# Decoder step with product-key experts: the value table taken one half of the width after the other, every product with w_hi on 448 columns, the first half's sums added midway

## What is computed

```python
def one(hx):                     # 128 rows at a time
    ...                          # top 16 of 128 x 128 product keys for 8 heads -> eidx, g = softmax(top)
    a = gelu(einsum('nd,nhkd->nhk', hx, u_tab[eidx]))
    w = (g * a)
    return einsum('nhk,nhkd->nd', w, v_tab[eidx])      # v_tab has 16384 rows of 1024
```

## Time and profile before

| | |
|---|---|
| three timed runs | 1252.82, 1248.13, 1249.46 us |
| profiled execution | 1249.17 us |
| its span, first to last instruction | 1247.5 us |
| TensorE busy | 1224.7 us, 98% |
| VectorE busy | 791.0 us, 63% |
| ScalarE busy | 623.3 us, 50% |
| GpSimd busy | 437.9 us, 35% |
| granted TensorE clock, mean | 0.991 |

### The profile page before, as it was taken

The page is one execution under the profiler, slowest core; times in us unless marked ns, Lnnn a source line. Parts: engine busy times, 40 slices in busy tenths (PEclk is TensorE's granted clock), DMA queues, the critical chain, the costliest instruction groups (busy, mean ns, idle before and its releaser), DMA issues.

```text
span 1247.5 us, 24718 instructions
## 1 busy us (share of the span) xinstructions
PE 1224.7 (98%) x9143; PEld 1141.2 (91%) x9143; DVE 791.0 (63%) x1425; ACT 623.3 (50%) x1265; POOL 437.9 (35%) x436
## 2 busy tenths in 40 slices
PE   7999999999999999999999999999999999999998
PEld 5688898978899999999999999999989898988988
DVE  6445565655784999997667777544555455545455
ACT  5333464532553544457777777544544444444443
POOL 3430325441000688883000000000556565565630
PEclk9999898999999999999999999999999999999999
DMA  8661836664655356565444444455788788888883
GB/s 324 209 202 53 129 124 221 222 204 140 203 193 167 108 159 184 160 181 165 137 144 130 141 135 137 147 175 182 285 263 304 266 301 273 295 275 291 287 281 121
DMA packets 104808, 246.90 MB, mean 198 GB/s; under 512 B 36080, under 2 KB 48432, under 8 KB 103984
## 3 DMA queue, kind: packets, MB, share of 16 engines
q1 hardware_dynamic: 78672, 190.51, 47.4%
q0 software_dynamic: 18752, 51.40, 12.5%
q10 hardware_dynamic: 7264, 3.40, 1.2%
HBM read 237.79 MB, written 11.64 MB: 200 GB/s over the span
## 4 chain that ended last, share of the span: by engine, by line
PE 89%; issue 2%; POOL 2%; DVE 2%; ACT 1%; SPq 1%; DMA 1%; ACTq 0%; DVEq 0%
PE ps L1975 23%; PE ps L1980 12%; PE ps L2065 9%; PE ps L2057 9%; PE ps L1539 5%; PE ps L2059 5%; PE ps L2060 4%; PE ps L2029 4%; PE ps L2078 2%; POOL w_lo L534 2%; PE ps L1792 2%; PE ps L1685 1%; PE ps L1559 1%; PE ps L1654 1%; PE ps L1647 1%
## 5 line engine op out<-in xcount | busy, mean ns | idle before, releaser
L882 ACT ACTIVATE w_hi<-ring 128x1024 fp32r<-128x1024 f32 x280 | 296.8, 1060 | 382.7 <-issue 212.8
L1338 DVE TENSOR_TENSOR w_lo<-ring,w_hi 128x1024 fp32r<-128x1024 f32 x232 | 283.9, 1224 | 278.1 <-ACT w_hi L882 278.1
L1975 PE MATMUL ps<-h_hi,w_hi 128*128 128x288 f32 x1088 | 299.9, 302 | 0.5 <-ACT w_hi L882 0.5
L1975 PE MATMUL ps<-h_lo,w_hi 128*128 128x288 f32 x1024 | 278.7, 296 | 0.0
L1975 PEld LDWEIGHTS ps<-h_hi,w_hi 128*128 128x128 f32 x1088 | 204.9, 188 | 1.2 <-ACT w_hi L882 1.0
L1975 PEld LDWEIGHTS ps<-h_lo,w_hi 128*128 128x128 f32 x1024 | 192.7, 188 | 0.0
L534 POOL TENSOR_TENSOR w_lo<-ring,w_hi 128x1024 fp32r<-128x1024 f32 x48 | 133.5, 2795 | 146.9 <-ACT w_hi L882 146.6
L550 POOL DMA_INDIRECT arena<-act_kept,aux x64 | 64.7, 1011 | 321.7 <-DMA act_kept<-arena 302.5
L543 POOL DMA_INDIRECT arena<-in_v,aux x128 | 134.6, 1051 | 111.4 <-PE ps L2078 76.4
L1980 PE MATMUL ps<-h_hi,w_lo 128*128 128x288 f32 x1088 | 166.7, 295 | 2.1 <-POOL w_lo L534 1.8
L1980 PEld LDWEIGHTS ps<-h_hi,w_lo 128*128 128x128 f32 x1088 | 152.5, 188 | 3.4 <-POOL w_lo L534 3.0
(11 more groups left out here) (361 smaller groups left out, 2287.9 us busy)
## 6 DMA issues: line engine op xcount, KB each, us to landing
ring<-in_uT SPq DMA_DIRECT2D x128, 512.0 KB, 3.6
ring<-in_v SPq DMA_DIRECT2D x128, 512.0 KB, 4.6
ring<-in_wout SPq DMA_DIRECT2D x32, 512.0 KB, 3.3
ring<-in_wT SPq DMA_DIRECT2D x28, 512.0 KB, 4.2
ring<-in_wtok SPq DMA_DIRECT2D x8, 512.0 KB, 4.0
arena<-in_cache_slc_v POOLq DMA_DIRECT2D x64, 64.0 KB, 2.9
act_kept<-arena SPq DMA_DIRECT2D x32, 128.0 KB, 3.8
arena<-in_cache_cmp_k POOLq DMA_DIRECT2D x48, 64.0 KB, 3.1
```

Of the source, the lines that this page charges most:

```text
L882: act.activation(w_hi[e % 2][:, :], ring[:, (W_O + e) % RING, :], ACT.Copy).then_inc(S["w_high"], 1)
L1338: dve.tensor_tensor(w_lo[e % 2][:, :], ring[:, (W_O + e) % RING, :], w_hi[e % 2][:, :].bitcast(F32), ALU.subtract)\
L1975: last = pe.matmul(ps[:, bank, 0:NT], w_hi[e % 2][:, k * P:(k + 1) * P], mov[:, k, :], start=(k == 0 and mov is mov_hi), stop=False, skip_ ...
```

## The change

Tile t now has dh = t // 64 and pp = t % 64: all 64 tiles of the left half of the width first, then all 64 of the right half. The right half's sums use banks 0 to 3 with 448 columns each, in place of two shared banks; banks 2 and 3 hold sums of the left half (m = 0 and 1), which are therefore added to `xT` in tile 64. Each tile has a moving operand of its own, so `mov_high` and `mov_low_part` are called for every tile, and tile t uses buffer t % 2. Cut to its core:

```diff
-VSUM = (((2, 0), (3, 0), (4, 0), (5, 0)), ((0, 0), (0, ND), (1, 0), (1, ND)))
+VBANK = ((2, 3, 4, 5), (0, 1, 2, 3))
 def v_tile(t):
-    pp, dh = t // 2, t % 2
+    pp, dh = t % HALF, t // HALF
...
             for a, b in ((0, 4), (4, 6), (6, 7), (7, 8)):
-                sp.wait_ge(S["y_ready"], b)
+                sp.wait_ge(S["y_ready"], b + 1)
...
-            def mov_high(pp):
-                if pp >= 2:
-                    act.wait_ge(S["lo_used"], E_V + 2 * (pp - 2) + 2)
-                    act.wait_ge(S["mov_low"], pp - 1)
-                act.activation(mov_parts[pp % 2][:, :, 0, :], rows[:, 2 * pp:2 * pp + 2, :], ACT.Copy).then_inc(S["mov_high"], 1)
+            def mov_high(t):
+                pp = t % HALF
+                if t >= 2:
+                    act.wait_ge(S["lo_used"], E_V + t - 1)
+                    act.wait_ge(S["mov_low"], t - 1)
+                act.activation(mov_parts[t % 2][:, :, 0, :], rows[:, 2 * pp:2 * pp + 2, :], ACT.Copy).then_inc(S["mov_high"], 1)
...
             act.wait_ge(S["tile_weighed"], PK - ROUTE_AT)
+            mov_high(1)
             for t in range(2, PK):
-                if t % 2 == 0:
-                    mov_high(t // 2)
+                mov_high(t)
                 w_high(E_V + t)
...
+            def add_sums(dh, ms):
+                for m in ms:
+                    dve.wait_ge(S["lo_used"], E_V + (HALF if dh == 0 else PK - 1 + m + 1))
+                    x = xT[:, 4 * dh + m, 0:ND]
+                    link(dve.tensor_tensor(x, x, ps[:, VBANK[dh][m], ND:2 * ND], ALU.add))
+                    dve.tensor_tensor(x, x, ps[:, VBANK[dh][m], 0:ND], ALU.add).then_inc(S["y_ready"], 1)
+            mov_low_part(1)
             for t in range(2, PK):
-                if t % 2 == 0:
-                    mov_low_part(t // 2)
+                if t == HALF + 1:
+                    dve.wait_ge(S["x1_back"], 32)
+                    add_sums(0, (0, 1))
+                mov_low_part(t)
                 w_low_part(E_V + t)
+                if t == HALF + 1:
+                    add_sums(0, (2, 3))
...
+            last.then_inc(S["y_ready"], 1)
+            add_sums(1, range(4))
...
                 pe.wait_ge(S["w_high"], e + 1)
-                pe.wait_ge(S["mov_low"], pp + 1)
-                for h in range(2):
-                    for m, (bank, c0) in enumerate(VSUM[dh]):
...
-                        pe.matmul(ps[:, bank, c0:c0 + ND], w, both[h][:, 0:ND], start=first, stop=False, skip_group_check=True)
-                        last = pe.matmul(ps[:, bank, c0:c0 + ND], w, both[h][:, ND:2 * ND], start=False, stop=False, skip_group_check=True)
+                pe.wait_ge(S["mov_low"], t + 1)
+                if t == HALF:
+                    high((0, 1))
+                    low_done(pe, e)
+                    low(0)
+                    low(1)
+                    pe.wait_ge(S["y_ready"], 2)
+                    high((2, 3)).then_inc(S["hi_used"], 1)
+                    low(2)
+                    low(3).then_inc(S["lo_used"], 1)
+                    return
+                high(range(4)).then_inc(S["hi_used"], 1)
...
-                if t == 1:
+                if t == HALF:
                     pe.wait_ge(S["u_done"], PK)
                     pe.wait_ge(S["tile_weighed"], PK - ROUTE_AT)
```

More of the change, by code:

```diff
@@ L1483, in weigh_tile, with mov_low_part @@
                 dve.tensor_tensor(rows[:, j, 0:cut], ps[:, j % 2, 0:cut], rows[:, j, 0:cut], ALU.mult).then_inc(S["tile_weighed"], 1)
[L1485 to L1490, removed]
+            def mov_low_part(t):
+                pp = t % HALF
+                dve.wait_ge(S["mov_high"], t + 1)
+                if t >= 2:
+                    dve.wait_ge(S["hi_used"], E_V + t - 1)
+                dve.tensor_tensor(mov_parts[t % 2][:, :, 1, :], rows[:, 2 * pp:2 * pp + 2, :], mov_parts[t % 2][:, :, 0, :].bitcast(F32), ALU.subtract)\
                     .then_inc(S["mov_low"], 1)
@@ L1522, in _ @@
                 new = ps[:, 6 + dh, :].rearrange("p (k q c) -> p k c q", k=4, q=GRP)[:, :, 0:EGROUPS, :]
[L1523 to L1531, removed]
+                last = dve.tensor_tensor(x, x, new, ALU.add)
+            last.then_inc(S["y_ready"], 1)
+            add_sums(1, range(4))
         @block.tensor
@@ L2045, in value_tile @@
             def value_tile(t):
-                pp, dh = t // 2, t % 2
+                dh = t // HALF
                 e = E_V + t
-                both = [mov[pp % 2][:, 2 * h * ND:2 * h * ND + 2 * ND] for h in range(2)]
-                pe.wait_ge(S["w_high"], e + 1)
-                pe.wait_ge(S["mov_low"], pp + 1)
-                for h in range(2):
-                    for m, (bank, c0) in enumerate(VSUM[dh]):
[L2054 to L2058, removed]
-                        pe.matmul(ps[:, bank, c0:c0 + ND], w, both[h][:, 0:ND], start=first, stop=False, skip_group_check=True)
-                        last = pe.matmul(ps[:, bank, c0:c0 + ND], w, both[h][:, ND:2 * ND], start=False, stop=False, skip_group_check=True)
@@ L2061, in value_tile, with high @@
-                last.then_inc(S["hi_used"], 1)
+                both = [mov[t % 2][:, 2 * h * ND:2 * h * ND + 2 * ND] for h in range(2)]
+                def high(ms):
+                    for h in range(2):
+                        for m in ms:
+                            last = pe.matmul(ps[:, VBANK[dh][m], 0:2 * ND], w_hi[e % 2][:, h * 512 + m * P:h * 512 + (m + 1) * P], both[h],
+                                             start=(t % HALF == 0 and h == 0), stop=False, skip_group_check=True)
+                    return last
@@ new lines, in low @@
+                def low(m):
+                    for h in range(2):
+                        last = pe.matmul(ps[:, VBANK[dh][m], 0:ND], w_lo[e % 2][:, h * 512 + m * P:h * 512 + (m + 1) * P], both[h][:, 0:ND],
+                                         start=False, stop=(t % HALF == HALF - 1 and h == 1), skip_group_check=True)
+                    return last
+                pe.wait_ge(S["w_high"], e + 1)
+                pe.wait_ge(S["mov_low"], t + 1)
[9 more added lines that the diff above has]
+                    return
@@ L2062, in value_tile @@
+                high(range(4)).then_inc(S["hi_used"], 1)
                 low_done(pe, e)
[L2063 to L2066, removed]
+                for m in range(4):
+                    last = low(m)
```

## The result

The changed kernel takes 1237.75 us, the median of 8 runs (1231.56 to 1243.01); the kernel before, run beside it, 1248.18 (1243.33 to 1252.82, 8 runs). The ratio is 0.992, with a 95% interval of 0.989 to 0.995: faster by 0.8%, 10.4 us between the medians. The forecast was 1241.9 us, between 1240.3 and 1246.0. The direction was right; the time lies 2.5 us under the range. The times alone couldn't tell a gain of 10.4 us from the forecast one of 7.3: that would be a ratio of 0.994, inside the interval. The traces can.

A forecast was written before the change was run, and what follows sets the result against it. TensorE's stream of matmuls was taken to set the pace. From one execution of 1249.17 us: - 8.8 (saving) + 0.6 (first tile) + 0.7 (tile 64) + 0.2 (end) = 1241.9 us, range for 8 in 10 1240.3 to 1246.

The forecast's parts named there:

- What bounds the kernel: Value stage: TensorE's stream of matmuls sets the pace, so what counts is the time from start to start.
- The saving: Right half's 64 tiles: merging 224-column matmuls into 448 saves 0.137 us a tile, 8.8 us in all, bounds 8.3 to 9.0.
- The fixed part of a matmul: Value stage matmuls: each costs 0.016 us besides its columns; the change takes 8 of these from each of 64 tiles.
- no fixed part: Rival, right half: the 0.111 us come from elsewhere, 448 columns keep 1.78 us; 1250.7 us, no change; chance 0.03.
- What is added in every tile: 62 more mov_high on ScalarE and 62 more mov_low on VectorE, covered by the tile before: cost nothing.
- First tile: Start of the value stage: tile 1 waits for its own mov_low after the last u tile's weighing; +0.6 us, bounds 0.5 to 0.9.
- tile 64: Between the halves: TensorE waits for two pairs of additions; +0.7 us, bounds 0.5 to 2.2.
- End: After tile 127's first w_lo matmul: later additions +0.8 us, stores -0.6; sum +0.2, bounds -0.3 to +0.8.
- The term for the stores: End of the span: 576 KB leave early, last store lands in 2.7 us; 2.9 us follow the last addition instead of 3.5, -0.6.
- Sum: Whole kernel: 1249.17 - 8.8 + 0.6 + 0.7 + 0.2 = 1241.9 us; with bounds 1240.9 to 1244.8.
- The Trainium skill's formula: Start to start of matmuls: 95.8 ns for 224 columns, 189.2 for 448; merging 512 pairs would save 1.2 us in all.
- the prediction's rival of the late ring: Rival, SP's tile loads: a load over 7.8 us delays a tile; one in ten late by 0.5 us gives 1248; chance 0.04.

The follow-up runs named there:

- e10: Changed kernel with w_hi of the right half in two matmuls of 224 columns instead of one of 448: 1249.1 against 1247.84 us, ratio 1.0006, stage 366.76 us.
- e9: Changed kernel with the right half's w_hi matmuls split into two of 224 columns for the second chunk h only: value stage 361.89 us.
- e6: Changed kernel with ScalarE making the first half of each moving operand's high parts twice: value stage 356.86 us, tiles 2.51 us.
- e7: Changed kernel with ScalarE making the whole high parts of each moving operand three times: value stage 388.9 us.
- e11: Changed kernel with mov_high(1) ahead of ScalarE's wait for the last weighed u tile and additions reordered with fewer waits: 1236.79 us, ratio 0.991.
- e2: Kernel before, with ScalarE's mov_high and w_high for tile t waiting for tile t - 2's last matmul: left tiles 2.54 us; stage 426.8, waiting for loads.
- e4: Changed kernel in the old paired order, all w_hi products 448 wide, without gathered rows' matmuls: 83 of 128 tiles 2.51 us; stage 367.4, waiting for loads.
- e5: Same edit as e11, run on the chip with late loads: 2.50 us from tile 1 to the next in place of 3.22; stage waited for loads.
- e1: Same edit as e10, run on the chip with late loads: ratio 1.000 to the kernel before, stage 448.9 us.
- e12: e11 with the right half's additions made two m by two m, on the chip with late loads: ratio 0.990, stage 401 us.

## Why the prediction was wrong, point by point

- **What bounds the kernel**: right. TensorE's starts set the pace in every tile, before and after.
- **The saving** (0.137 x 64 = 8.8 us): that the merged matmuls carry it was right, shown by e10 and e9, but the term was sized too small. It took the left tile's 2.54 us as what every tile would take. All-wide tiles take 2.51. The gross saving is 366.24 - 356.38 + 0.70 + 0.79 = 11.4 us: 64 right tiles gained 0.167 each (10.7), the left ones the rest. This is the first failing step, and the one that counts: a tile's time was taken from a mixed sequence to one without the mixture. The range of the term, 8.3 to 9.0, held only the reading error of two differences, not that. Why all-wide tiles are faster stays open.
- **The fixed part of a matmul** (0.016 us): the line through 224 and 448 columns gives what a merged pair saves, but the rows of other widths don't bear out a fixed part. They show a floor of 0.11 us, so the rival *no fixed part* (0.03) had that half right; its other half, that 448 columns would keep 1.78 us, was wrong.
- **What is added in every tile**: cost nothing, as argued; e6 shows the room in ScalarE's chain, e7 that the room ends, at a lower price than I gave.
- **First tile** 0.6, measured 0.70; **tile 64** 0.7, measured 0.79, both by the chain of instructions that was named, and removable as named (e11 for the first).
- **End**: the additions as forecast (3.39 against 3.34). The term for the stores (-0.6) was too small; the second failing step. I kept 2.7 us to landing although the queue would be idle. It was 1.7 us, and the sum of the end is -0.5, outside my bounds of -0.3 to +0.8.
- **Sum**: -7.3 forecast, -10.4 measured, 3.1 us apart: 11.4 - 8.8 = 2.6 from the saving, 0.7 from the end, less 0.2 for the two gaps.
- **The starting point**: I summed from one execution of 1249.17 us. The kernel before has a median of 1248.18 over 8 runs. With -10.4 that gives 1237.8, the measured time; with my -7.3 it would give 1240.9, inside the range. So 1.0 us of the distance to the forecast is the base, which moves with the clock in the first 300 us.
- **The Trainium skill's formula** ("TensorE: Matmul & The Clock Gate", Back-to-back issue gap, N / 2.4 + 2.5 ns, which that section calls the gap of an isolated matmul) gave 1.2 us for the merging; e10 against the changed kernel gives 10.4. The measurement decides, as it did in the trace before.

## What to carry to other kernels

Matmuls that each load 128 columns of weights didn't follow each other faster than every 0.11 us here, with 34 columns or with 224, so one of 448 columns beats two of 224 by 0.02 us each time; that is worth banks and a second conversion of the moving operand as long as the other engines have the room. Don't take the 0.02 us to other widths: read both spacings from a trace. Don't carry a duration from a mixed sequence to a uniform one without widening its bounds, and look whether the same instruction has several spacings already: the 2.51 us tiles stood in the trace before. And where runs scatter, compare the changed stretch of the traces, not the spans.

## What had not been expected of the hardware

- The floor of 0.11 us between matmuls with new weights, from 34 to 224 columns.
- Wide matmuls with the same shapes follow each other in 0.204 us (w_hi part 1.63) or in 0.207 (1.66), by what ran before them, not by waits (e2, e4). The cause is open.
- With loads at the same places, one chip moved less than another: in the stage of e5 247 GB/s with TensorE busy 88.92 of 100 us and its clock at 0.97, against 294 GB/s in the changed kernel on another chip. In e5 TensorE's loads of weights wait 54.9 us for w_hi, up to 6.0 us at once, which fits late loads; that trace doesn't give their landing. It isn't the prediction's rival of the late ring, since the kernel before is slower on that chip by about as much, and variants keep their ratios there (e1 1.000 as e10, e12 0.990 beside e11's 0.991).

**e5**, 1100 to 1200 us:

```profile
1100.00:1200.00 100.00, 88.92 (x553) 76.29 (x552) 55.62 (x65) 45.69 (x60) 52.59 (x49) 0.97 0.72 247
```

**changed kernel**, the same window:

```profile
1100.00:1200.00 100.00, 100.00 (x652) 87.20 (x645) 66.66 (x77) 54.01 (x71) 61.84 (x56) 1.00 0.86 294
```

- GpSimd's gathers mostly take longer beside VectorE's added instructions: L543 1169 ns on average, against 1051 before, with GpSimd's wait for TensorE down from 76.4 to 57.4 us. The Trainium skill ("SBUF — State Buffer", Who interferes with whom) has VectorE instructions with two inputs in SBUF contend with GpSimd's reads, which agrees in sign. Denser transfers aren't the cause: e10 has the pace of before (283 GB/s from 880 to 1220 us, 284 before) and a gather takes 1188 ns. But e6 has the same added VectorE instructions at 288 GB/s, and only 1073 ns, so these instructions alone don't explain it; what does is open.
